# MLA attention: the division of the softmax weights on ScalarE instead of GpSimd

## What is computed

```python
logits = jnp.einsum('bqhd,bkhd->bhqk', qblk, k).astype(jnp.float32) * scale
p = jax.nn.softmax(logits, axis=-1).astype(v.dtype)
return jnp.einsum('bhqk,bkhd->bqhd', p, v)
```

## Time and profile before

| | |
|---|---|
| median of three runs | 1801.13 us (1800.45, 1801.13, 1807.62) |
| the profiled execution | 1804.88 us, its span 1803.1 us |
| TensorE busy | 1710.0 us (95%) |
| VectorE, ScalarE, GpSimd busy | 998.3, 746.4, 855.5 us |
| mean granted TensorE clock | 0.988 |
| attention stage | from about 350 to 484 us of the span |

### The profile page before, as it was taken

How to read it: one execution, slowest core, us unless ns; L and a number is a source line. 1 busy time by engine, 2 the same in 40 slices (tenths; PEclk the granted TensorE clock), 3 DMA queues, 4 the chain that set the end, 5 groups by cost and what they waited for, 6 DMA issues and landing times.

```text
span 1803.1 us, 25317 instructions
## 1 busy us (share of the span) xinstructions
PE 1710.0 (95%) x10068; PEld 1435.4 (80%) x10068; DVE 998.3 (55%) x1622; ACT 746.4 (41%) x1151; POOL 855.5 (47%) x491
## 2 busy tenths in 40 slices
PE   5999999999899999999999998999978999999997
PEld 2888777655587889999999995777766879889886
DVE  2133345666567866464645679760187885333354
ACT  2531223655434853232333346442435583333344
POOL 1342212066536366455554651343335757566475
PEclk9999999999999999999999999999989999999999
DMA  9312242255412121212122243322201323333231
GB/s 349 89 47 59 59 140 94 98 172 174 142 47 71 47 71 51 85 53 82 59 77 65 71 132 111 109 67 59 70 1 47 94 70 118 94 94 116 72 117 59
DMA packets 189515, 163.81 MB, mean 91 GB/s; under 512 B 17742, under 2 KB 168494, under 8 KB 189398
## 3 DMA queue, kind: packets, MB, share of 16 engines
q1 hardware_dynamic: 187616, 160.92, 29.2%
q10 hardware_dynamic: 1782, 1.28, 0.2%
HBM read 160.08 MB, written 2.10 MB: 90 GB/s over the span
## 4 chain that ended last, share of the span: by engine, by line
PE 80%; DVE 12%; ACT 3%; issue 2%; DMA 1%; SPq 1%; POOL 0%; POOLq 0%; ACTq 0%; DVEq 0%
PE ps L1036 37%; PE ps L1024 10%; PE ps L1026 10%; PE ps L1025 10%; PE ps L1236 2%; PE ps L1261 2%; PE ps L1357 1%; PE ps L1145 1%; PE ps L988 1%; PE ps L1246 1%; PE ps L1161 1%; DVE lnbuf L2595 1%; DMA mod_rest<-in_mod_w 1%; SPq L852 1%; DVE xT L2584 1%
## 5 line engine op out<-in xcount | busy, mean ns | idle before, releaser
L3214 POOL TENSOR_TENSOR wsplit<-wsplit_raw,wsplit 128x512 fp32r<-128x512 f32 x108 | 149.9, 1408 | 118.4 <-DVE wsplit_raw L2753 105.6
L2584 DVE SCALAR_TENSOR_TENSOR xT<-ps,modc,xT 128x512 f32<-128x512 f32 (+1 forms) x168 | 104.1, 657 | 150.0 <-PE ps L1036 128.0
L1036 PE MATMUL ps<-us_a,wsplit 128*128 128x512 f32 x864 | 179.8, 355 | 3.1 <-DVE us_a L2854 1.7
L3199 POOL TENSOR_TENSOR wsplit<-ring,wsplit 128x1024 fp32r<-128x1024 f32 (+1 forms) x48 | 112.4, 2352 | 112.3 <-ACT wsplit L1918 112.3
L1036 PEld LDWEIGHTS ps<-us_a,wsplit 128*128 128x128 f32 x864 | 142.2, 188 | 27.7 <-DVE us_a L2854 2.4
L1036 PE MATMUL ps<-h,wsplit 128*128 128x512 f32 x720 | 156.0, 377 | 1.0 <-DVE hu L2677 1.0
L1930 ACT ACTIVATE wsplit<-wsplit_raw 128x512 fp32r<-128x512 f32 x108 | 68.4, 633 | 203.9 <-DVE wsplit_raw L2753 203.9
L1036 PE MATMUL ps<-us_b,wsplit 128*128 128x512 f32 x720 | 151.1, 354 | 1.7 <-DVE us_b L2854 1.7
L1036 PEld LDWEIGHTS ps<-h,wsplit 128*128 128x128 f32 x720 | 127.8, 188 | 26.1 <-DVE hu L2677 1.2
L3214 POOL TENSOR_TENSOR wsplit<-ring,wsplit 128x512 fp32r<-128x512 f32 x81 | 115.4, 1437 | 61.0 <-ACT wsplit L1930 61.0
L1036 PEld LDWEIGHTS ps<-us_b,wsplit 128*128 128x128 f32 x720 | 118.4, 188 | 21.5 <-DVE us_b L2854 2.1
(11 more groups left out here) (495 smaller groups left out, 3957.0 us busy)
## 6 DMA issues: line engine op xcount, KB each, us to landing
ring<-in_ffn_w_in SPq DMA_DIRECT2D x88, 512.0 KB, 3.8
ring<-in_mod_w SPq DMA_DIRECT2D x77, 512.0 KB, 4.5
ring<-in_ffn_w_out SPq DMA_DIRECT2D x40, 512.0 KB, 3.4
ring<-in_m_w_in SPq DMA_DIRECT2D x24, 512.0 KB, 3.7
ring<-in_ab_w_in SPq DMA_DIRECT2D x21, 512.0 KB, 3.9
mod_rest<-in_mod_w SPq DMA_DIRECT2D x10, 512.0 KB, 15.7
ring<-in_ab_w_out SPq DMA_DIRECT2D x8, 512.0 KB, 4.2
ring<-in_m_w_out SPq DMA_DIRECT2D x8, 512.0 KB, 3.9
```

The lines of the kernel that those rows point to most:

```text
L1036: mm = pe.matmul(dst[:, a:b], w, h[:, a:b], start=st, stop=sp_)
L2584: ins = dve.scalar_tensor_tensor(xT[:, m, a:b], pair[:, a:b], modc[:, l, g, m, v:v + 1], xT[:, m, a:b], ALU.mult, ALU.add)
L3199: pool.tensor_tensor(down_unit(l, g, q, 1), down_ring(l, g, q), down_unit(l, g, q, 0).bitcast(F32), ALU.subtract).then_inc(lo_made, 1)
L3214: pool.tensor_tensor(w_op(l, p, o, 1), src, w_op(l, p, o, 0).bitcast(F32), ALU.subtract).then_inc(s_lo, 1)
```

## The change

ScalarE gets a function `att_normalise` that multiplies the weights of an item by the reciprocal of their sum, in place, with a Copy activation whose scale is a per-partition column. It is issued for item i-1 behind the exponential of item i and ahead of att_high. GpSimd's loop of 48 multiplications is gone. The semaphores att_r and att_p are the same; att_r is now waited for by ScalarE, and att_p is signalled by it.

```diff
+        def att_normalise(it):
+            act.wait_ge(att_r, it + 1)
+            a = 0 if it % TT < LT else LAT
+            act.activation(probs(it)[:, a:T], probs(it)[:, a:T], ACT.Copy, scale=den[:, 1, it:it + 1]).then_inc(att_p, 1)
+
         def att_copy(it):
...
             if i < N_ATT:
                 att_exponent(i)
+            if 1 <= i <= N_ATT:
+                att_normalise(i - 1)
             if i % TT == 1 and i // TT + 1 < H_MLA:
                 att_high(i // TT + 1)
...
-        for i in range(N_ATT):
-            pool.wait_ge(att_r, i + 1)
-            a = 0 if i % TT < LT else LAT
-            pool.tensor_scalar(probs(i)[:, a:T], probs(i)[:, a:T], den[:, 1, i:i + 1], None, ALU.mult).then_inc(att_p, 1)
         split_out_low(0, 0)
```

## The result

The changed kernel takes 1813.53 us (median of four runs, 1809.3 to 1814.76), the kernel before 1801.96 beside it (four runs, 1800.45 to 1807.62). The ratio is 1.0049, with a 95% interval of 1.0027 to 1.007: the change costs some 9 us, and 5 to 13 is possible. (The two medians of four runs lie 11.6 us apart, a quotient of 1.0064; four runs don't tell more than the interval does.) A second measurement of the same two kernels, 11 runs against 34, gave 1811.28 against 1802.99: 1.0046 [1.0031, 1.006], which is 8.3 us. The forecast was 1805.0, no measurable difference. The sign is the forecast's and the size is twice its 3.9 us.

The account below looks back on a forecast made before the run. TensorE was taken to bound the attention stage, with only 12.8 us of standing. Late high parts (2.6 us) and late copies (1.3 us) summed to 3.9 us on the median of 1801.13, forecasting 1805.0, range 1800 to 1812.

Parts of the forecast that it names:

- What bounds the kernel: Attention stage: TensorE sets the pace, busy 121.2 of 134.0 us; GpSimd's division is hidden, so removing it frees nothing.
- The added instruction: ScalarE's division: 0.92 us for 768 columns, 0.83 of queue time; ScalarE rises from 70 to 103 busy us, not the bound.
- the rival with 1880 us: ScalarE's Copy needs table loads of 1.28 us around it, some 78 us over 32 latent turns; chance 0.02.
- Term 1, the high parts: Division ahead of att_high delays VectorE's low parts and TensorE: three uncovered places at 0.83 us plus 0.1, 2.6 us.
- Term 2, the copy: ScalarE's att_copy starts late behind values blocks and low parts, delaying TensorE's next transpose: 0.8 + 0.5 = 1.3 us.
- Term 3, the end: Last division delays the first split for the output projection by at most 0.4 us; covered, so it costs nothing.
- The sum: Delays in the attention stage total 2.6 + 1.3 = 3.9 us, forecast 1805.0; chance 0.60.
- The clock: Rival: longer TensorE stalls drop its clock to 0.50, four falls costing 6.4 us more, time 1811.4; chance 0.14.
- more stretches at clock 0.50: Sign that the forecast is wrong: TensorE's granted clock at 0.50 more often between 350 and 484 us.
- The rival that all is hidden: The delay ends in a later wait that TensorE has anyway: time 1801 to 1802; chance 0.14.
- The rival that VectorE is freed: VectorE's low parts no longer held by GpSimd's divisions, three chains give back 3.0 us: time 1802.0; chance 0.06.

Follow-up runs that it names:

- fillers: 256-column TensorE products nobody reads, placed where it stands: on the changed kernel 1.0015, on the kernel before 1.0004, both against the kernel before.
- changed, again: The changed kernel measured a second time with no edit, against the kernel before: 1811.28 against 1802.99 us, ratio 1.0046.
- GpSimd busy: The changed kernel, with GpSimd still multiplying 48 tiles from another source into an unused tile: ratio 1.0032 to the kernel before.
- idle work in turn 1: The kernel before plus a 768-column ScalarE Copy into an unread tile ahead of att_high, at seven places: ratio 1.0021.
- the division skipped there: The changed kernel without the seven divisions ahead of att_high, those items staying undivided: ratio 1.0000 to the kernel before.
- the low parts in two turns: The kernel before with VectorE's att_low cut in two, keys in turn 2 of a head and queries in turn 3: ratio 0.9972.

## Why the prediction was right or wrong

**What bounds the kernel: right.** TensorE's 12.8 us of standing were the frame, and GpSimd's division was hidden: without any division the ratio is 0.9995.

**The added instruction: right.** It lasts 0.93 us (forecast 0.92), overlaps the next by 0.1 (374.44 to 375.26 is 0.82, forecast 0.83), and ScalarE is busy 101.1 us in the stage (forecast 103). No table load appears in the stage, no product of TensorE's waits for a division (one weight load does, 0.9 us, in the second profile), and ScalarE does not become the bound, so the rival with 1880 us is out.

**Term 1, the high parts: right, 2.62 us for 2.6.** The three bare places passed on 0.83, 0.84 and 0.83, the fourth 0.12, and the three ahead of the blocks of values nothing. The cause is shown from both sides: seven idle instructions bring 3.8 us in, and seven divisions fewer take the loss out. One detail differs: the stall of 0.95 us grew to 1.71 at turns 10 and 34, but at turn 4 it was the wait of 0.81 us for the exponential that grew.

**Term 2, the copy: right in kind, slightly large.** 0.31, 0.35, 0.21 and 0.2 make 1.1 us for 1.3. The place behind the middle block cost nothing, as forecast.

**Term 3, the end: right.** The projection is as late as the last block of values, 6.62 us, and not more.

**The sum: the step that failed is what it left out.** The terms give 3.7 us in the trace for 3.9, but the runs show 8.3 (5.6 to 10.8). The clock stood as a rival with a chance of 0.14, "One fall more (1806.6) is likelier than four", and the sum held nothing for it. It should have been a term. In the profiled pair it is 2.3 us of 6.0, 1.3 of them from a fall that the second profile does not have. Over all runs the mean granted clock fell from 0.9866 (96 runs of the kernel before) to 0.9836 (11 runs), and fillers that leave each late operation late give 5.6 us back.

What the clock costs on average can be estimated from the kernel before alone. Among its 34 runs of the group of "changed, again" a run takes 1.0 us longer for each 0.001 that its mean clock is lower (a straight line through time and clock, correlation -0.84). By that line 3.4 of the 8.3 us are the clock, and at equal clock the changed kernel is 4.9 us slower, within about 1.3, where 3.9 was forecast. The others, each against the line of its own group, fit: 4.8 us at equal clock with the fillers, 4.9 with GpSimd busy, 2.0 with idle work in turn 1, 2.1 with the division skipped there, each good to about 1 us. So the terms of standing were right within that uncertainty, and the missing term was worth some 3.4 us. The prediction had named it among its own signs of being wrong, "more stretches at clock 0.50".

The rival itself was half right. Its four new falls are not in the trace; one fall twice as long as before and one new one are, which is the "one or two falls (1806 to 1809)" that held most of its chance. Its price of half the length is an upper bound, since a part lies in stalls: 3.35 us by the granted clock, 2.3 us of delay. And its condition, that one stall of 1.8 us is enough, does not hold each time: the stall of 1.71 us ahead of 380.09 left the clock at 1.00 until 390, so did the one ahead of 449.15 in the second profile, and without a division the one ahead of 364.50. The kernel before had such a stall too, ahead of 361.75, inside the fall of rows 14; the prediction counted only the stalls of 0.95.

**The rival that all is hidden** falls with the 3.7 us of standing losses. **The rival that VectorE is freed** falls with the low parts of 0.95 us in either case, and with GpSimd kept busy at 1.0032.

**The chances.** The sign was the forecast's, but the size sat on the clock's 0.14 and not on the 0.60 of the sum; that the range held is owed to the room left for four falls, which did not come. The range of 1800 to 1812 counts from a median of 1801.13; 8.3 us on it is 1809.4 and a ratio of 1.0049 is 1810.0, both inside, and inside the bound of 0.5%. The median of the four runs itself, 1813.53, lies 1.5 us above the top.

**Open.** Turn 1's share is 3.8 us when added alone and 8.3 when left out. At equal clock these are 2.0 and 2.8 (4.9 less 2.1), either side of the 2.6 of the trace, so the clock seems to make most of the gap. Why the clock falls in one execution and not in another is not shown. How far fillers help by the clock alone rests on one kernel; the number of falls differs between executions of one kernel, so a profile shows a fall and not its average cost.

## What to carry to other kernels

An instruction put on a half-idle engine costs what stands behind it in that engine's queue: 41 of the 48 divisions cost nothing on ScalarE that the ratio shows (1.1 us in the trace), and seven, ahead of operands that a chain of VectorE and TensorE waited for, cost what could be measured of the loss. So look for a place behind what others wait for, and expect a rest (2.7 us were left here, because the division was then late itself). Look first whether the work taken away was hidden (here 85 us of it), because then there is only something to lose. A stall that a change lengthens on a full TensorE can be priced twice, once as standing and once by the clock behind it, and the same bare chain may be worth cutting in the kernel before: that gave 5 us where the change cost 8.

## What the runs showed of the hardware

TensorE's clock does not follow the program alone. The 34 runs of the kernel before in one group have mean granted clocks from 0.982 to 0.991, and of two profiles of the changed kernel one has a fall near 450 us and the other has not. Of the profiled stages, the kernel before lost 1.75 us to it, the one without divisions none, and the one with the low parts in two turns 5.10, though that is the fastest of the kernels without fillers. One of the falls of that last kernel came behind a single stall of 0.75 us, in a stretch otherwise full (timeline, then busy time):

```profile
450.79 0.65 PE L998 MATMUL ps<-kc,mrow 2*128 2x2 f32 x8 [0.75 <-DVE mrow L2361]
```

```profile
446.00:450.00 4.00, 4.00 (x32) 2.48 (x32) 2.98 (x8) 2.66 (x6) 2.20 (x1) 1.00 0.80 242
...
452.00:456.00 4.00, 4.00 (x14) 1.56 (x15) 2.16 (x6) 0.82 (x2) 3.31 (x2) 0.59 0.02 6
```

In the changed kernel a fall began inside a stall, before any work came: TensorE stood from 361.51 to 363.21, and from 362.00 to 363.20 the granted clock was 0.50.

```profile
362.00:363.20 1.20, 0.00 (x0) 0.02 (x1) 1.06 (x2) 0.57 (x2) 0.00 (x0) 0.50 0.11 44
```

And useless products can pay: twelve of them made the changed kernel some 5.6 us faster and its mean clock 0.9884 for 0.9836, while six made the kernel before no faster. Last, GpSimd and VectorE did not slow each other: 0.95 us for VectorE's subtraction with GpSimd multiplying and with GpSimd idle, and 2.20 us for GpSimd's multiplication beside it.
